# Attention scores of an encoder layer: the second 128-row product of each 512 keys becomes half of a pair of 64-row products

## The reference, cut to what matters

```python
sc = jnp.einsum('bqhcd,bkhcd->bhcqk', qi, k, preferred_element_type=jnp.float32) * scale
p = jax.nn.softmax(sc, axis=-1)
w = p[:, :, 0] - lam * p[:, :, 1]
return jnp.einsum('bhqk,bkhd->bqhd', w.astype(v.dtype), v)
```

## Time and profile before

| | us |
|---|---|
| median of 3 runs | 2987.74 (2984.97 to 2989.3) |
| profiled execution, its own time | 2983.51 |
| its span, first to last instruction | 2981.5 |
| PE busy in it | 2843.7 |
| DVE busy in it | 2275.6 |

### The profile page before, as it was taken

The page is one execution under the profiler, slowest core; times in us unless marked ns, Lnnn a source line. Parts: engine busy times, 40 slices in busy tenths (PEclk is TensorE's granted clock), DMA queues, the critical chain, the costliest instruction groups (busy, mean ns, idle before and its releaser), DMA issues.

```text
span 2981.5 us, 40161 instructions
## 1 busy us (share of the span) xinstructions
PE 2843.7 (95%) x13947; PEld 2390.5 (80%) x13947; DVE 2275.6 (76%) x3066; ACT 1345.9 (45%) x2442; POOL 1534.6 (51%) x1153
## 2 busy tenths in 40 slices
PE   7999998999999998999899999999999999999896
PEld 3888886666666665888899998999899997878785
DVE  5666665988888874566787789898888775688787
ACT  3111112777777774456643343334433443233454
POOL 0233321011111124567767676777776766577797
PEclk9999999999999998999999999999999999999998
DMA  7444347121312105466543454555454367587763
GB/s 264 123 141 126 115 139 181 43 71 57 84 57 71 50 22 175 147 198 226 201 152 116 129 175 167 199 179 179 145 170 160 125 201 269 198 283 272 251 208 117
DMA packets 324772, 460.88 MB, mean 155 GB/s; under 512 B 23318, under 2 KB 207319, under 8 KB 318554
## 3 DMA queue, kind: packets, MB, share of 16 engines
q1 hardware_dynamic: 324572, 458.32, 47.4%
HBM read 308.98 MB, written 149.24 MB: 154 GB/s over the span
## 4 chain that ended last, share of the span: by engine, by line
PE 37%; DVE 9%; DVEq 5%; POOL 4%; DMA 3%; issue 2%; POOLq 1%; ACT 1%; SPq 0%; ACTq 0%
PE tail_bank L2515 6%; PE tail_bank L2516 6%; PE tail_bank L2517 6%; PE tail_bank L2533 4%; PE tail_bank L2534 4%; PE tail_bank L2535 4%; DMA tail_plain<-in_w_dn 2%; DVE tail_plain L2718 2%; PE tail_bank L2455 1%; PE tail_bank L2453 1%; PE tail_bank L2454 1%; POOL tail_rounded L2267 1%; DVE tail_plain L2684 1%; DMA tail_plain<-scr_dn_d 1%; POOL tail_plain L2304 1%
## 5 line engine op out<-in xcount | busy, mean ns | idle before, releaser
L2267 POOL TENSOR_TENSOR tail_rounded<-tail_plain,tail_rounded 128x512 fp32r<-128x512 f32 x462 | 670.5, 1481 | 281.9 <-ACT tail_rounded L2031 281.9
L2515 PE MATMUL tail_bank<-tail_rounded 128*128 128x384 f32 x1848 | 624.5, 338 | 26.8 <-DVE tail_rounded L2666 17.2
L2516 PE MATMUL tail_bank<-tail_rounded 128*128 128x384 f32 x1848 | 622.4, 337 | 0.0
L2517 PE MATMUL tail_bank<-tail_rounded 128*128 128x384 f32 x1848 | 622.0, 337 | 0.0
L2031 ACT ACTIVATE tail_rounded<-tail_plain 128x512 fp32r<-128x512 f32 x462 | 273.7, 624 | 484.1 <-DVE tail_plain L2652 385.4
L2515 PEld LDWEIGHTS tail_bank<-tail_rounded 128*128 128x128 f32 x1848 | 350.4, 190 | 32.9 <-issue 17.6
L2516 PEld LDWEIGHTS tail_bank<-tail_rounded 128*128 128x128 f32 x1848 | 350.8, 190 | 0.0
L2517 PEld LDWEIGHTS tail_bank<-tail_rounded 128*128 128x128 f32 x1848 | 350.7, 190 | 0.0
L1154 DVE TENSOR_REDUCE att_peak<-att_sc 128x1 f32<-128x1024 f32 x256 | 312.8, 1222 | 41.9 <-PE att_sc L966 35.3
L1058 ACT ACTIVATE att_e<-att_sc,att_peak 128x1024 f32<-128x1024 f32 x256 | 285.4, 1115 | 81.8 <-DVE att_peak L1162 81.8
L2533 PE MATMUL tail_bank<-tail_rounded 128*128 128x512 f32 x693 | 275.0, 397 | 21.6 <-DVE tail_rounded L2724 11.8
(11 more groups left out here) (290 smaller groups left out, 5495.8 us busy)
## 6 DMA issues: line engine op xcount, KB each, us to landing
tail_plain<-in_w_gu SPq DMA_DIRECT2D x134, 512.0 KB, 4.9
scr_a_d<-tail_plain SPq DMA_DIRECT2D x231, 192.0 KB, 2.1
tail_plain<-scr_a_d SPq DMA_DIRECT2D x85, 256.0 KB, 5.2
scr_out_d<-tail_plain SPq DMA_DIRECT2D x18, 1024.0 KB, 5.0
tail_plain<-scr_out_d SPq DMA_DIRECT2D x18, 1024.0 KB, 7.0
proj_ada<-in_w_ada SPq DMA_DIRECT2D x16, 1024.0 KB, 6.9
held_w_hi<-scr_qs_d SPq DMA_DIRECT2D x128, 128.0 KB, 2.9
scr_h_d<-tail_plain SPq DMA_DIRECT2D x63, 256.0 KB, 4.3
```

Of the source, the lines that this page charges most:

```text
L2267: nc.gpsimd.tensor_tensor(w_lo[:, j, :], operand(F, j), w_hi[:, j, :].bitcast(F32), ALU.subtract).then_inc(wlo_done, 1)
L2515: nc.tensor.matmul(dst, w_hi[:, j, cols], h_hi(b, j)[:, k, :], start=(k == 0), stop=False)
L2516: nc.tensor.matmul(dst, w_hi[:, j, cols], h_lo(b, j)[:, k, :], start=False, stop=False)
L2517: m = nc.tensor.matmul(dst, w_lo[:, j, cols], h_hi(b, j)[:, k, :], start=False, stop=(k == 3))
```

## The change

Three things change. First, key tiles with an odd chunk number (each chunk is 512 keys) get their halves swapped: low in partitions 0 to 63, high in 64 to 127. For that each key transfer is cut in two, since its even and odd chunks now go to different partitions. Second, for a half's two chunks c = 0 and 1 the first product is now the one that holds the two cross terms: form 1 for the even chunk, form 0 for the odd one, over 128 partitions. Third, the other product is replaced by high·high over 64 partitions: partitions 0 to 63 for c = 0, partitions 64 to 127 for c = 1, one behind the other, into different banks. The term low·low is no longer computed. The prompt steps keep their two 128-row products.

```diff
@@ load_attention
-                        sp.dma_start(w_hi[part * QK:(part + 1) * QK, at:at + 2, 0:512].bitcast(F32),
-                                     ks_d[0, part, i // 2][:, keys].rearrange("c (q t) -> c q t", q=2)).then_inc(k_first[i], 16)
+                        for odd in range(2):
+                            rows = slice((part ^ odd) * QK, (part ^ odd) * QK + QK)
+                            sp.dma_start(w_hi[rows, at + odd, 0:512].bitcast(F32),
+                                         ks_d[0, part, i // 2][:, keys][:, odd * 512:(odd + 1) * 512]).then_inc(k_first[i], 16)
@@ load_k
-                        sp.dma_start(w_hi[part * QK:(part + 1) * QK, 4 * mp:4 * mp + 4, head % 2 * D:head % 2 * D + 512].bitcast(F32),
-                                     ks_d[head, part, mp][:, PROMPT:].rearrange("c (q t) -> c q t", q=4)).then_inc(k_landed[head % 2], 16)
+                        for odd in range(2):
+                            rows = slice((part ^ odd) * QK, (part ^ odd) * QK + QK)
+                            sp.dma_start(w_hi[rows, 4 * mp + odd:4 * mp + 4:2, head % 2 * D:head % 2 * D + 512].bitcast(F32),
+                                         ks_d[head, part, mp][:, PROMPT:].rearrange("c (q t) -> c q t", q=4)[:, odd::2, :]).then_inc(k_landed[head % 2], 16)
@@ scores
                     tokens = slice(N % 2 * P, (N % 2 + 1) * P)
+                    dst = [sc[:, x % 3, c * 512:(c + 1) * 512] for c in range(2)]
+                    keys = [keys_at(w_hi, N // ST, mp, 2 * h + c) for c in range(2)]
+                    queries = [queries_at(w_hi, N // 2, form, mp)[:, tokens] for form in range(2)]
                     for c in range(2):
-                        dst = sc[:, x % 3, c * 512:(c + 1) * 512]
-                        keys = keys_at(w_hi, N // ST, mp, 2 * h + c)
-                        nc.tensor.matmul(dst, queries_at(w_hi, N // 2, 0, mp)[:, tokens], keys, start=True, stop=False)
-                        m = nc.tensor.matmul(dst, queries_at(w_hi, N // 2, 1, mp)[:, tokens], keys, start=False, stop=True)
+                        nc.tensor.matmul(dst[c], queries[1 - c], keys[c], start=True, stop=False)
+                    for c in range(2):
+                        high = slice(c * QK, (c + 1) * QK)
+                        m = nc.tensor.matmul(dst[c], queries[c][high], keys[c][high], start=False, stop=True)
                 m.then_inc(s_done, 1)
```

More of the change, by code:

```diff
@@ L954, in scores @@
                     if N == 0:
-                        pe.wait_ge(k_first[2 * mp + h], 32)
+                        pe.wait_ge(k_first[2 * mp + h], 64)
                     if mp == 0 and h == 0:
@@ L959, in scores @@
                         if N and N % ST == 0:
-                            pe.wait_ge(k_landed[N // ST % 2], 64 * ((N // ST + 1) // 2))
+                            pe.wait_ge(k_landed[N // ST % 2], 128 * ((N // ST + 1) // 2))
                     tokens = slice(N % 2 * P, (N % 2 + 1) * P)
+                    dst = [sc[:, x % 3, c * 512:(c + 1) * 512] for c in range(2)]
+                    keys = [keys_at(w_hi, N // ST, mp, 2 * h + c) for c in range(2)]
+                    queries = [queries_at(w_hi, N // 2, form, mp)[:, tokens] for form in range(2)]
                     for c in range(2):
-                        dst = sc[:, x % 3, c * 512:(c + 1) * 512]
-                        keys = keys_at(w_hi, N // ST, mp, 2 * h + c)
-                        nc.tensor.matmul(dst, queries_at(w_hi, N // 2, 0, mp)[:, tokens], keys, start=True, stop=False)
-                        m = nc.tensor.matmul(dst, queries_at(w_hi, N // 2, 1, mp)[:, tokens], keys, start=False, stop=True)
+                        nc.tensor.matmul(dst[c], queries[1 - c], keys[c], start=True, stop=False)
+                    for c in range(2):
+                        high = slice(c * QK, (c + 1) * QK)
+                        m = nc.tensor.matmul(dst[c], queries[c][high], keys[c][high], start=False, stop=True)
                 m.then_inc(s_done, 1)
```

## The result

The changed kernel takes 3009.39 us (median of 4, 3005.1 to 3011.22) against 2986.6 before (median of 4), a ratio of 1.0072 with a 95% interval of 1.0057 to 1.0088. It is slower by some 21 us. Its profiled execution has a span of 3003.0 us against 2981.5.

A forecast was written before the change was run, and what follows sets the result against it. Attention was taken as bound mostly by DVE and ACT's chain, not PE; -4.9 (y and z waits) - 1 (other waits) + 2 (way in) = -3.9 us, so 2979.6 profiled, 2983.8 as median; range 2963 to 3010.

The forecast's parts named there:

- a plain TensorE bound: Mid-attention read as limited by PE alone: one score product less per quarter would give 50 us over 54 steps.
- a round gains two times what a half gains: Attention, four steps: only the steps with y and z gain, each once what one half of scores gets shorter.
- 25.8 us: Attention: most that faster scores can give, 13.5 rounds of 1.91 us waiting, called about a third of 50 us.
- The 0.2 us for that slack: Mid-attention: PE's idle time in a round of four steps, taken from 0.77 us idle in 140 us.
- DVE's own 8.63: Attention: the shortest step, 8.63 us, taken as what DVE alone needs, without a gap or wait for PE.
- my first two terms: Attention: shorter waits in steps with y and z, -4.9 us, and DVE's irregular and early waits, -1 us.
- What a half gets shorter: Score products: pair side by side saves 0.23 us, two shape changes cost 0.05, so a half is 0.18 shorter.
- The pair side by side: Score products: the two 64-row products run beside each other, holding PE for one product's 0.23 us.
- The drain: Score products: emptying the array at two shape changes, side estimate 0.11 us per half, sum -2.2 instead of -3.9.
- The slower rival: Score products: serial pair or unhidden weight loads, each half 0.18 us longer, 3028 us; decides above 0.92 us; chance 0.22.
- The way in: Loads before attention: 16 more transfers cost SP 5.2 us, partly absorbed, +2 us; extra issues inside attention hidden.
- Clock: First attention steps: clock might stay at 0.50 (1.2 GHz), up to +3 us over four steps; taken as 0.

The follow-up runs named there:

- e1: Kernel before with three 128-row products per half, the odd chunk's second form left out (two terms missing), no pair, old loads: 2978.33 us, ratio 0.9971.
- e10: Changed kernel with each chunk's 64-row product right behind its own 128-row product, four changes of array shape per half instead of two: 3185.40 us, ratio 1.0657.
- e6: Kernel before with each chunk's second product given 64 weight columns instead of 128, all 128 rows, issued behind both first products: 2986.90 us, ratio 0.9998.
- e4: Changed kernel with both 64-row products on partitions 0 to 63, so they can't run side by side: 3080.81 us, ratio 1.0317.
- e7: Changed kernel with only one of the two 64-row products, that of the odd chunk: 3010.93 us, ratio 1.0079.
- e12: Changed kernel with 64 weight columns instead of 128 in each 64-row product, still two changes of array shape per half: 2998.78 us, ratio 1.0030.
- e2: Kernel before with each key transfer cut in two as in the changed kernel, every part to its old place, products as before: 2991.17 us, ratio 1.0010.
- e3: Changed kernel's products on the loads of the kernel before, keys of odd chunks not swapped: 3010.54 us, ratio 1.0077.
- e5: Changed kernel with the pair of 64-row products issued twice per half, still two changes of array shape: 3065.12 us, ratio 1.0262.

## Why the prediction was wrong, point by point

- **What bounds the stage.** That PE's 99% hides a stage in which faster scores are worth little was right: e1, with the full 0.23 us saved per half, gave 8 us of the 50 that a plain TensorE bound promises. (The 25.8 us that I called a third of these 50 are half of them.) That a round gains two times what a half gains was right too, by e1's steps. Right only in one direction, though. I had written myself that PE has little slack in a round, so it gives little when it gets faster and takes most when it gets slower. The 0.2 us for that slack, from PE's busy time, was too low: of 16 × 0.12 = 1.92 us a round grew by 1.29, and in e10 of 16 × 0.74 = 11.8 by 11.0, so some 0.6 to 0.8 us are absorbed.
- **DVE's own 8.63.** Wrong by 0.23: it held a hidden wait for PE. With e1's 0.23 in place of 0.18 my first two terms give -7.2 us; this step is worth 13.5 × 0.23 = 3.1 more.
- **What a half gets shorter.** This is the step that failed: "a shape change costs 0 to 0.09, a half 0 to 0.18. I take 0.05 for both together". Measured 0.35 for both. I took a change of columns for a change of rows. e6 shows the first costs nothing, e10 that the second costs about 0.2 each. The half became 0.12 us longer in place of 0.18 shorter, and a round 1.29 longer: 17.4 us where I had -4.9.
- **The pair side by side.** Right: e4 and e7 show the second product free. The Trainium skill's page TensorE: Matmul & The Clock Gate says the same in Part 3: Packing small matmuls — row/col tiling, and the traces agree.
- **The drain.** The Trainium skill's page TensorEngine Tiling warned in Key Properties that changing the mode drains the engine. Beside the sum I had an estimate from the drain alone, 0.11 us for two changes. The traces agree with the warning for rows (0.35, three times that estimate); for columns (e6) nothing was paid, and whether 64 weight columns count as another mode no run tells. What the estimate lacked is, by the starts of the loads and by e12, at least in part the weight load that isn't hidden across the change. The Trainium skill's page TensorE: Matmul & The Clock Gate, in LDWEIGHTS (loading the stationary operand), makes a load go by its columns; an estimate from its formula is 53 ns for the 64 columns that e12 leaves out, and e12's records show 0.05 us.
- **The slower rival.** It had the right sign, and with its weights that "can't be loaded beside the product before" the mechanism that the traces bear out best, with a chance of 0.22; but it priced the half as if the pair were also serial, 3028 us. The real case lies between: pair side by side, changes dearer than it saves. Its point of decision, a half above 0.92 us, was right. With the measured 0.12 its sum gives about +27 us in place of the 22.7 at step 62, because of the slack. That 3009.39 lies inside the range is luck: the top of 3010 came from cutting off half of this case, not from a mechanism.
- **The way in.** +2 forecast, about right. Sixteen issues took 10.10 us and PE's first score came at 499.65, as I had written. The first maxima came 1.7 us later; e2 measured about 3 us, its interval from 0 to 6. The extra issues inside attention cost nothing, as forecast: e2's 54 steps took 505.7 us, the kernel before 505.5.
- **Clock.** I took 0 with up to +3. The stretch up to 521 us ran at 0.50, and step 1 was reached 4.2 us late (523.72 against 519.53), of which 2.5 are not in the late start. e3, whose first score came 0.5 us before that of the kernel before, has the same low clock and is 3.3 us late at step 8. How much of this is the clock and how much the longer half, no run takes apart.

## What to carry to other kernels

A 64-row product between 128-row products costs two changes of the array's row shape, 0.35 to 0.41 us here, more than the 0.23 us that a pair side by side saves. Such pairs can pay only where several of them stand together or all neighbours have the same shape: two in a row would save 2 × 0.23 - 0.35 = 0.11 us of PE's time, an estimate from e5 and the changed kernel that no run tried. Price a change of shape from a row of the same kind of change, and if there is none, keep the range open above what the pair could save. An engine at 99% that gains little from less work may still lose most of what more work costs: here 1.29 of 1.92 us a round.

## What was not expected of the hardware

- 64 rows and 64 columns are not alike: the next weights are not loaded ahead across a change of rows (about 0.2 us per change), and a change of columns costs nothing (0.01 us per quarter at most, interval of the ratio 0.9985 to 1.0011).
- A single 64-row product costs as much as two side by side, 0.43 us, and a second pair inside the shape only 0.23.
- At the start of a stage the clock didn't follow the length of the wait ahead of it: back at 505 behind 8.68 us (e2), only at 521 or 522 behind 8.83 (changed kernel) and 5.18 (e3). Three 128-row products behind 5.31 us (e1) stayed at 0.50 to about 516 as well, so what decides is not shown.
- In e4 PE was busy in all of 530 to 570 us, and the clock was at 0.50 until about 579. e5, with the same quarter, had the full clock from 524.
